# Two transformer blocks on one core: from a list of stages to one order of mixed steps, with the context tokens as a stream of their own

## The reference, cut to what matters

```python
# block 1, tokens x (512 x 1024)
p = rmsnorm(x) @ w_in            # 15 tiles of 128 channels for q and k, and v
ya, yc, yd = softmax attentions  # 12 heads: biases from a table, causal or a window of 128
yb = stick_breaking_attention    # 4 heads: log-sigmoids, a suffix sum, exp
x += group_rmsnorm([ya, yb, yc, yd]) @ w_out
x += softmax(rmsnorm(x) w_xq, keys from 256 memory tokens) @ w_xo
x += square(relu(rmsnorm(x) @ w_up)) @ w_down ;  x = rmsnorm(x)
# block 2, twice (l = 0, 1); modulation vectors from silu(c) @ ada_w (1024 x 6144 each)
h = modulate(rmsnorm(x)) ; hc = modulate(rmsnorm(ctx))
q, k = rope(rmsnorm over 64 channels) ; context keys and queries without rope
a = softmax(q1 k1) - lam * softmax(q2 k2)        # 8 heads, 768 keys
y_b = rmsnorm(a v) ; y_a = gelu(u) * mix(layernorm(gelu(va))) ; y_c = gb * dwconv3(gc * xin)
x += g1 * ((sig_a * (y_a wa) + sig_b * (y_b wb) + sig_c * (y_c wc)) @ wo)
x += g2 * ((silu(conv g) * conv val) @ ffn_down) # 2816 hidden channels
# layer 0 does all of that for ctx as well; layer 1 takes only keys and values from it
```

## Time and profile before

| | us |
|---|---|
| Median of three executions (4232.05, 4233.14, 4260.79) | 4233.14 |
| The profiled execution, its own time | 4241.65 |
| Its span, first to last instruction | 4239.9 |
| PE busy | 3775.1 (89%) |
| DVE busy | 1499.9 (35%) |
| ACT busy | 847.1 (20%) |
| GpSimd busy | 1459.6 (34%) |
| Mean granted clock of PE | 0.912 of 2.4 GHz |

### The profile page before, as it was taken

How to read it: one execution, slowest core, us unless ns; L and a number is a source line. 1 busy time by engine, 2 the same in 40 slices (tenths; PEclk the granted TensorE clock), 3 DMA queues, 4 the chain that set the end, 5 groups by cost and what they waited for, 6 DMA issues and landing times.

```text
span 4239.9 us, 45936 instructions
## 1 busy us (share of the span) xinstructions
PE 3775.1 (89%) x19290; PEld 3120.2 (74%) x19290; DVE 1499.9 (35%) x2807; ACT 847.1 (20%) x1517; POOL 1459.6 (34%) x880
## 2 busy tenths in 40 slices
PE   5994768999799798989999899997997998998999
PEld 4752556888689466878888788887894677877887
DVE  1142235885201885012212441422008811333332
ACT  1036322110202353011001220211013511012111
POOL 3500121656132000333433234442430034654664
PEclk9987767999797997999998899997989989998999
DMA  2200022775011000111111111211210012222232
GB/s 105 88 20 5 31 79 74 255 262 185 20 60 45 1 1 1 60 65 50 60 60 50 40 60 65 70 52 44 80 45 1 1 60 75 93 86 70 88 106 85
DMA packets 50351, 285.85 MB, mean 67 GB/s; under 512 B 5546, under 2 KB 5930, under 8 KB 25827
## 3 DMA queue, kind: packets, MB, share of 16 engines
q1 hardware_dynamic: 45648, 269.93, 18.8%
q10 hardware_dynamic: 4498, 12.99, 0.8%
HBM read 280.77 MB, written 2.13 MB: 67 GB/s over the span
## 4 chain that ended last, share of the span: by engine, by line
PE 78%; DVE 14%; issue 4%; ACT 3%; DMA 1%; ACTq 0%; DVEq 0%; SPq 0%
PE ps L257 20%; PE ps L263 20%; PE ps L259 20%; PE ps L638 6%; DVE small L1215 3%; PE ps L322 2%; PE ps L321 2%; PE ps L320 2%; DVE diff_p L1208 2%; PE ps L867 1%; PE ps L891 1%; DVE diff_p L1206 1%; PE ps L866 1%; PE ps L1029 1%; DVE hlo L770 1%
## 5 line engine op out<-in xcount | busy, mean ns | idle before, releaser
L1649 POOL CAST whi<-raw 128x1024 fp32r<-128x1024 f32 (+1 forms) x438 | 447.7, 1022 | 2723.0 <-DMA raw<-in_w 2723.0
L257 PE MATMUL ps<-hhi,whi 128*128 128x512 f32 x2656 | 953.6, 359 | 115.2 <-issue 80.6
L1651 POOL TENSOR_TENSOR wlo<-raw,whi 128x1024 fp32r<-128x1024 f32 (+1 forms) x438 | 1024.1, 2338 | 35.1
L259 PE MATMUL ps<-hlo,whi 128*128 128x512 f32 x2656 | 905.8, 356 | 0.0
L263 PE MATMUL ps<-hhi,wlo 128*128 128x512 f32 x2656 | 796.0, 357 | 0.0
L257 PEld LDWEIGHTS ps<-hhi,whi 128*128 128x128 f32 x2656 | 506.3, 191 | 239.3 <-issue 82.7
L259 PEld LDWEIGHTS ps<-hlo,whi 128*128 128x128 f32 x2656 | 506.1, 191 | 73.1
L263 PEld LDWEIGHTS ps<-hhi,wlo 128*128 128x128 f32 x2656 | 442.8, 192 | 32.7
L257 PE MATMUL ps<-h1hi,whi 128*128 128x512 f32 (+1 forms) x488 | 195.1, 400 | 53.6 <-ACT marks L1674 52.5
L1326 DVE CUSTOM_DVE_ANT_0 ada_out<-ada_w,ps 128x1024 f32<-128x1024 f32 x192 | 222.3, 1215 | 0.0
L1144 PE MATMUL ps<-k,q 64*128 64x256 f32 (+1 forms) x576 | 185.6, 528 | 13.5 <-ACT diff_p L1182 9.3
(11 more groups left out here) (258 smaller groups left out, 5650.8 us busy)
## 6 DMA issues: line engine op xcount, KB each, us to landing
raw<-in_w SPq DMA_DIRECT2D x187, 1024.0 KB, 4.9
ada_w<-in_ada SPq DMA_DIRECT2D x96, 512.0 KB, 4.5
raw<-in_w SPq DMA_DIRECT2D x32, 704.0 KB, 4.0
x<-in_x ACTq DMA_DIRECT2D x1, 3072.0 KB
att_toe<-toe_dram ACTq DMA_DIRECT2D x12, 256.0 KB, 3.1
out<-x ACTq DMA_DIRECT2D x1, 2048.0 KB, 7.2
cond<-in_cc ACTq DMA_DIRECT2D x1, 1024.0 KB
memx<-in_mem ACTq DMA_DIRECT2D x1, 1024.0 KB
```

The source lines that it names most:

```text
L257: nc.tensor.matmul(o, whi[:, buf, b:b + P], self.hi[:, k, n0:n1], start=(k == 0), stop=False)
L259: nc.tensor.matmul(o, whi[:, buf, b:b + P], self.lo[:, k, n0:n1], start=False, stop=False)
L1649: nc.gpsimd.tensor_copy(whi[:, buf, c0:c1], raw[:, buf, c0:c1]).then_inc(half_hi, 1)
L1651: nc.gpsimd.tensor_tensor(wlo[:, buf, c0:c1], raw[:, buf, c0:c1], whi[:, buf, c0:c1].bitcast(F32), ALU.subtract).then_inc(half_split, 1)
```

## The change

The whole program is reordered and its parts are rewritten to stand it. (1) The marks and the stage list go. All parts are cut into steps (mostly one output tile, one attention half-unit, one head), and one list `order` gives the steps of all engines; each engine runs its share of each step in that order and waits only for the data it reads. (2) The context is a stream of its own with 256-wide tiles. Layer 0's work for it stands between the steps of block 1's attentions, and layer 1's context keys and values after block 1; the keys and values pass through DRAM. Each layer-0 weight is therefore loaded and split twice. (3) In block 2 the attention and its norm are woven with the gating unit's two input projections (`u`, `va`), the gating unit, and the branches a and c; branch b comes last. (4) The norm over 64 channels and the rotation move into the epilogue of the q and k projections (`QKHeads`). Norms sum squares by a product with a 128 x 128 constant, so root and reciprocal run over full rows. (5) Sigmoid becomes Tanh with halved gates. (6) The modulation products stand half in the first projection and half in the squared-ReLU network. (7) Slabs have 8 blocks, the ring 5 slots. (8) The attention of block 2 keeps both rows of scores of a unit in one place in PSUM. (9) `x` is loaded in four parts from SP and the result stored by tiles.

The core of the diff:

```diff
-BLOCKS = 16
+BLOCKS = 8
+RING = 5
-RING = 3
...
-        def block_ready(pe, slab, b):
-            if b in (0, 8):
-                pe.wait_ge(half_split, 2 * slab + 1 + b // 8)
...
+        def place(part, i):
+
+            if i == 0:
+                part.begin()
+            part.place(i)
+            order.append((part, i))
...
+        def weave(main, filler):
+
+            at_ = 0
+            for n, (part, i) in enumerate(main):
+                place(part, i)
+                upto = (n + 1) * len(filler) // len(main)
+                for other, j in filler[at_:upto]:
+                    place(other, j)
+                at_ = upto
...
+        def feature_tile(pe, tile, slab, b0, kt, hi, lo, n, ready=None):
+
+            bank_ready(pe, tile)
+            o = pb(tile % 2, n)
+            for k in range(kt):
+                s, b = slab[(b0 + k) // BLOCKS], (b0 + k) % BLOCKS
+                if b == 0 or k == 0:
+                    pe.wait_ge(slab_split, s + 1)
+                if ready is not None:
+                    pe.wait_ge(*ready(k))
+                c = slice(b * P, (b + 1) * P)
+                buf = s % RING
+                nc.tensor.matmul(o, whi[:, buf, c], hi[:, k, 0:n], start=(k == 0), stop=False)
+                nc.tensor.matmul(o, whi[:, buf, c], lo[:, k, 0:n], start=False, stop=False)
+                mm = nc.tensor.matmul(o, wlo[:, buf, c], hi[:, k, 0:n], start=False, stop=(k == kt - 1))
+            mm.then_inc(tile_done, 1)
+
...
+        class QKHeads(Epilogue):
...
+                    nc.tensor.matmul(self.mixes[m % 2], self.swaps, self.raws[m % 2], start=True, stop=True)
+                nc.tensor.matmul(self.stats[m % 2], blocks64, self.sq[m % 2], start=True, stop=True).then_inc(self.mm, 1)
...
+                    nc.scalar.activation(self.stats[m % 2], self.stats[m % 2], ACT.Sqrt,
+                                         bias=cst[:, EPS_COL:EPS_COL + 1]).then_inc(self.rt, 1)
...
+                    nc.vector.reciprocal(self.stats[m % 2], self.stats[m % 2]).then_inc(self.rr, 1)
...
+                    nc.vector.scalar_tensor_tensor(self.dst(m), self.out(m), self.gain, self.rope[:, 0, :],
+                                                   ALU.mult, ALU.mult).then_inc(self.free(m), 1)
...
+                    nc.vector.tensor_tensor(mix, mix, self.rope[:, 1, :], ALU.mult).then_inc(self.qs, 1)
+                    dve.wait_ge(*freed(self.g.tile[m]))
+                    dve.wait_ge(self.qs, self.qs0 + 2 * m + 1)
+                    nc.vector.tensor_tensor(d, mix, d, ALU.add).then_inc(self.qs, 1)
+                    dve.wait_ge(self.qs, self.qs0 + 2 * m + 2)
+                    dve.wait_ge(self.rr, self.rr0 + m + 1)
+                    nc.vector.tensor_tensor(d, self.stats[m % 2], d, ALU.mult).then_inc(self.qo, 1)
...
-        class Norm:
...
-                        mm = nc.tensor.matmul(st[:, o:o + self.nh], sq[:, c * P:(c + 1) * P],
-                                              halves if self.nh == 2 else ones, start=(k == 0 and c == 0),
-                                              stop=last, skip_group_check=True)
...
+        class Norm(Part):
...
+                nc.tensor.matmul(self.stats[g], spread(self.mean), self.sq[k % 2], start=(k == self.group.index(g)),
+                                 stop=(k == self.K - 1 or self.group[k + 1] != g)).then_inc(self.sum, 1)
...
+                    for s in self.stats:
+                        v = nc.vector.reciprocal(s, s)
                     v.then_inc(self.rr, 1)
...
+        class SubNorm(Part):
...
+                    nc.vector.reciprocal(r, r).then_inc(self.rr, 1)
...
+        class DiffAttention(Part):
...
+                    if a == 1:
+                        pe.wait_ge(self.ex, self.ex0 + v)
+                    elif self.pn0 + t:
+                        pe.wait_ge(self.pn, self.pn0 + t)
+                    r = slice(HD * a, HD * a + HD)
+                    for n0, n1 in ((0, 512), (512, TT)):
+                        mm = nc.tensor.matmul(pb(2, n1 - n0, n0), self.q[r, h, i * P:(i + 1) * P],
+                                              self.k[r, h, n0:n1], start=True, stop=True)
+                    mm.then_inc(self.s, 1)
...
+        class Branch(Part):
...
+                    nc.scalar.activation(self.G[m % len(self.G)], pb(t % 2, self.n), ACT.Tanh, scale=0.5)\
+                        .then_inc(tile_free[t % 2], 1)
...
+        x = zone("x", [P, KT, T], 0)
+        hhi = zone("hhi", [P, KT, T], 16, F32R)
+        hlo = zone("hlo", [P, KT, T], 32, F32R)
+        xc = zone("xc", [P, KT, TC], 48)
+        chi = zone("chi", [P, KT, TC], 56, F32R)
+        clo = zone("clo", [P, KT, TC], 64, F32R)
...
+        run(norm_mix, tables, spread0)
+        weave(steps(project, values_c, *values), steps(ada0))
+        run(Modulation(0))
+        context = [n1c, val_c, key_c, store_c, query_c, att_c, sub_c, b_c, u_c, va_c, load_sgu_c, sgu_c, a_c, conv_c, c_c]
+        context_order = steps(*context)
+        context_order += [(o_c, i) for i in range(o_c.steps)] + [(n2c, i) for i in range(n2c.steps)]
+        context_order += steps(*ffn_c)
+        weave(steps(softmax, stick), context_order)
+        run(reload, load_mem, norm_group)
+        weave(steps(out_proj), steps(norm_mem))
+        run(keys_x, values_x, norm_cross, query_x, xatt, split_x)
+        then_norm(out_x, norm_mlp)
+        run(spread1)
+        weave(steps(*mlp[0:3]), steps(ada1))
+        run(Modulation(1))
+        then_norm(mlp[3], norm_final)
+        for l, L in enumerate(layers):
+            if l == 0:
+                run(L["norm1"])
+                run(n1c1, val_c1, key_c1, store_c1)
+            run(L["rotate"], L["loads"], L["sgu_load"])
+            run(L["q"], L["k"], L["v"])
+            main = []
+            for t, step in enumerate(steps(L["att"])):
+                main.append(step)
+                if t >= 12 and (t - 12) % 8 == 0:
+                    main.append((L["sub"], (t - 12) // 8))
+            main += [(L["sub"], i) for i in range(L["sub"].steps) if (L["sub"], i) not in main]
+            filler = steps(L["u"], L["va"], L["sgu"], L["a"], L["conv"], L["c"])
+            weave(main, filler)
+            run(L["b"])
+            then_norm(L["o"], L["norm2"])
+            run(L["up"])
+            if l + 1 < LAYERS:
+                then_norm(L["down"], layers[l + 1]["norm1"])
+            else:
+                run(L["down"])
...
+            for j in range(4):
+                sp.dma_start(x[:, 2 * j:2 * j + 2, :], x_in[:, 2 * j:2 * j + 2, :]).then_inc(x_loaded[j], 16)
...
-            for n, stage in enumerate(stages):
-                if n not in joined and n:
-                    pe.wait_ge(act_stage, begun(n))
-                    pe.wait_ge(dve_stage, begun(n))
-                for part in stage if isinstance(stage, list) else [stage]:
-                    part.tensor(pe)
+            for part, i in order:
+                part.tensor(pe, i)
...
```

2826 lines of the change are left out of this document (1596 added, 1230 removed).

## The result

The changed kernel takes 4385.24 us (median of four runs, 4380.17 to 4389.46) against 4237.82 for the kernel before (median of four executions, one more than in the table above): 1.0337 times as long, 95% interval 1.0295 to 1.0379. The forecast was 3910, faster. The profiled run (4380.17 us) is set against the forecast sum of 3917.

The account below looks back on a forecast made before the run. PE was taken to bound the kernel, waiting for ACT and DVE at a fallen clock in norms and block 1's attentions. Parts from start 42 to layers 1149 and 1132 summed to 3915, hence 3910 on the median's scale; range 3700 to 4110.

Parts of the forecast that it names:

- A unit's own chain: Block 2's woven attention: one unit's scores, maxima, exponentials and DVE steps take about 9.8 us, hidden behind filler tiles.
- rival A: Whole kernel: chains hide wholly because ACT and DVE run ahead, 3670 us; chance 0.17.
- 52 of additions: Woven part of a layer: 15 table loads, 28 reciprocals and 9 gating unit on top of 404, making 456 us.
- the 28 for the reciprocals that hold DVE: Woven part: eight head norm reciprocals hold DVE, 5.7 us a head, adding 28 us.
- The 15 for table loads: Woven part: 15 us added where Gelu and Exp force two table loads a step.
- The 174: Block 2's attention run unwoven, taken at its old stage's 174 us, within 469 unwoven against 456 woven.
- Block 1, 800: Block 1's softmax and stick-breaking attentions with the context's work woven in: 800 us.
- The floor of 662 and the 137 of chains: Block 1 with the context: PE work of 662 us plus 137 for chains in which steps wait for one another.
- First projection, 137: First projection: PE needs 130 us, DVE's 111 of modulation steps beside its copies end last, 137 in all.
- D: Rival: the 512-wide reciprocal is dearer (4109 us) or cheaper (3840) than the line; upper end shares chance 0.14 with B.
- C: Rival: table loads on PE's path, 317 if Tanh shares no table with Exp; 4246 or 4334 us; chance 0.05.
- B: Rival: chains set the pace in woven parts, 469 to 500 us a layer, 4109 total; chance 0.14 shared with D's upper end.

Follow-up runs that it names:

- head norm behind: Changed kernel with block 2's norm over heads run after the attention's last step, fillers spread over both: 4338.47 us, ratio 1.0249.
- second place: On top of the norm moved after the attention, each of a unit's two score rows gets its own place in PSUM: 4237.77 us, ratio 1.0011.
- half steps behind: On the kernel with two score places, the norm after the attention cut in half steps, last 20 filler steps between them: 4200.64 us, ratio 0.9927.
- the same, with block 1's even spread and half steps: Adds context steps spread evenly over block 1's attention steps (4189.81 us), then the context's norm over heads in half steps: 4176.93 us, ratio 0.9864.
- deeper order: On the 4176.93 us kernel, a unit's transposes half a step later and its values one unit later: 4114.13 us, ratio 0.9709.
- the best form: The 4114.13 us kernel with the second row's exponential in SBUF, 4115.09 us; against it, block 2's attention unwoven took 4198.57.
- the deep one: The 4115.09 us kernel with block 2's attention alone in front of its fillers, transposes and values at the old distances: 4198.57 us, ratio 0.9919.
- the fastest kernel: Two score places, half-step head norms, even block 1 spread, transposes half a step and values one unit later: 4114.13 us, ratio 0.9709.

## Why the prediction was wrong

**The woven parts: the step that failed** is "A unit's own chain is scores 2.55, two maxima and two exponentials 3.7, [...] with small steps about 9.8", of which the prediction says "It is hidden behind 5.48 tiles, and only just behind the 2.7 ones". The chain's length was about right. What I did with it was not: I compared one length with one sum of PE work. In a strict order a unit is cut into two half steps, and PE must find each wait's answer ready at its own place. With one place for the scores the first row's maximum and exponential must fit before the second row, and the second row's exponential and both DVE steps before the next unit; where no filler tile stood between, or a head norm did, PE stood. The diff shows all of it: a wait of the second row on `ex`, one place, one copy of the transposed probabilities, values a unit earlier. I named the one place among the changes, and among the reasons against rival A, and gave it no price. The sum has 52 us beyond PE's 404; in the changed kernel PE was idle 96 and busy 486.

The experiments, each on top of the one above it, price the step. Woven part in us:

| | layer 0 | layer 1 |
|---|---|---|
| changed kernel | 582 | 582 |
| head norm behind | 563 | 558 |
| second place | 510 | 507 |
| half steps behind | 490 | 493 |
| the same, with block 1's even spread and half steps | 491 | 490 |
| deeper order | 458 | 456 |

Of the 126 us in layer 1, 79 are idle time of PE (96 to 17) and 47 products that run faster (486 to 439, the clock from 0.87 to 0.99).

**The 456 at the end is the forecast's number, but not its sum; that it fits is in part luck.** The forecast was 404 of PE work and 52 of additions. The measured part is 439 busy and 17 idle. So at a clock of 0.99 PE's floor is 35 us more than I had, and the additions were 35 too dear. Among these, the 28 for the reciprocals that hold DVE came to 5 to 8 us a layer when they were taken away. The 15 for table loads cannot be more than a part of the 17: 41 loads stand in that part.

**The 174** of "unwoven the same steps are 174" failed the same way. It is the time of a stage of the old form. The new form takes 414 alone, 276 with a second place, 193 to 206 with its distances back. From it I concluded that weaving gives near nothing (469 against 456). It gave the changed kernel 4741 - 4385 = 356 us, and 83 in the best form.

**The clock.** The forecast had block 2's stretches near 1.0, as in the earlier trace rows. I treated the clock as a property of a stage. In these runs it moved with the waits: 0.87 in the woven part, 0.99 in the same products with most waits gone, 0.52 to 0.68 in the unwoven attentions with short distances. A wait cost its length and then slower products. How much slower, the total of the waits does not tell: layer 1's unwoven attention with two places and the deep one are both idle 26 us (274 less 248, 199 less 173), at 0.68 and 0.97. The gaps differ: most are 0.8 to 1.6 us in the first, 0.5 to 0.75 in the second. Whether that is what decides is not shown. And the prediction's "0.50 to 0.57 of full in the norms" leaves out the first norm, whose row has 1.00.

**Block 1, 800 against 938.** The floor of 662 and the 137 of chains were judged for the whole. Measured are 748 of busy time, at a clock of 0.84, and 190 of idle time, so both fell short. The experiments name two terms that the sum had at nothing: the spread, 25 (the context's attention had one softmax step to three or four of its own), and GpSimd beside DVE, 28. The table loads of the stick-breaking steps are worth 35, but the sum had 50 for those steps with their loads, so they are no missing term. Some 85 of the 138 stay open, and that the two add is not shown. I had also set GpSimd aside by its sum (531 us of 800), while the rows of one half slab and one context tile, 3.36 against 2.88, say that it is last wherever the context runs by itself; woven, PE waits for it only some 3 us in the last 403.

**First projection, 137 against 162.** DVE's 125 us beside the copies was foreseen; that PE would wait 15.6 us for copies of the short value tiles, because each copy stands behind a modulation step, was not. DMA moved 238 GB/s there.

**What held.** Reciprocals of 512 columns take 3.36 us (forecast 3.54), of 256 columns 1.76 (1.79), so D is out. The q and k tiles are 7.3 us apart (7.2). The 362 of the feed-forward became 375, with the tail of the norm in it. Table loads are 179, fewer than my 205 and far from C's 317, and each 1.28 us with 0.1 to 0.5 of idle before most groups. C is out: the fastest kernel has 41 of them in a woven part in which PE is idle 17 us in all. The trace again disagrees with the 2.66 us a switch of the Trainium skill (ScalarE: Activation LUTs, "What ACT_TABLE_LOAD costs"). Its advice to batch by table set ("Table sets: the hidden batching unit") bears on the 35 us in block 1. Of the signs of being wrong that I had named, one came in part: PE waited 96 us in a woven part and not 60, but 43 of them for Exp or pn and 52 for the head norm.

**The rivals.** B had the right mechanism, but with 469 to 500 a layer it borrowed the 174 too, so its 4109 fell short as well. The one place could have been priced from the diff: 2 x (1.27 + 0.96 + 0.15 + 1.1) + 2.2 = 9.2 us a unit at the full clock, 295 for 32 units and not 174. The measured unit is 13.45; two rows of scores at 2.9 and not 1.27 are 3.3 of the 4.3 us between. Nothing was measured for A: 3670 needs chains that hide wholly.

## What to carry to other kernels

When a stage is cut into steps and woven, price each wait at its place in the order: what the instruction needs, and how many us of other work stand between, half step by half step; an average over the part hides it. A time measured for the old form of a stage is no price for the new one when buffers or distances shrink with it. Weave last: first give every producer one step of distance to its consumer (a second place in PSUM, transposes half a step later), then, in these runs, the same filler tiles hid nearly all of the chain.

## What the runs showed of the hardware

- PE busy to 90% is not PE at speed: in the unwoven attention with two places waits of about 1 us between groups went with a clock of 0.68, and 150 us of products took 248. The same attention at the old distances had 0.90 and 0.97, in layer 1 with the same 26 us of idle time in all.
- GpSimd's stream slows DVE where DVE works from SBUF: a scaling of 768 columns took 0.61 us alone, 0.92 on average in a woven part beside both GpSimd operations, 0.69 beside its cast only. Maxima from PSUM stayed at 0.96.
- It matters more with two operands in SBUF: the same subtraction of 768 columns took 1.02 us with one of its rows in PSUM and 1.73 on average with both in SBUF, in woven parts with the same GpSimd work (155 and 157 us). Unwoven, with GpSimd at 8 us of the window, the form with both in SBUF took 1.04. Without GpSimd's subtraction the head norm's subtraction of 512 columns, both operands in SBUF, fell from 1.37 to 0.69.
- 53 table loads, each 1.28 us, were taken away; 0.66 us each came back in the section's time.
